# W11 pieces copied on chip into the down projection's running sum, and two W21 pieces added by GpSimd

## What is computed

```python
for l in range(DEPTH):
    x = x + hybrid_mixer(x, ...)
    x = x + conv_ffn(x, ffn_norm[l], w_up[l], conv_w[l], conv_b[l], w_down[l])
return rms_norm(x, final_norm)

def conv_ffn(x, norm_g, w_up, conv_w, conv_b, w_down):
    ...
    return (jax.nn.silu(a) * b) @ w_down      # (512, 2816) @ (2816, 1024)
```

## Time and profile before

| | |
|---|---|
| median of 3 runs | 1578.74 us (1578.1 to 1582.06) |
| time of the profiled execution | 1583.04 us |
| its span, first to last instruction | 1581.2 us |
| TensorE busy | 1563.6 us (99%) |
| VectorE, ScalarE, GpSimd busy | 74%, 49%, 16% |
| mean granted TensorE clock | 0.997 |
| DMA moved | 231.41 MB, 146 GB/s over the span |

### The profile page before, as it was taken

How to read it: one execution, slowest core, us unless ns; L and a number is a source line. 1 busy time by engine, 2 the same in 40 slices (tenths; PEclk the granted TensorE clock), 3 DMA queues, 4 the chain that set the end, 5 groups by cost and what they waited for, 6 DMA issues and landing times.

```text
span 1581.2 us, 22764 instructions
## 1 busy us (share of the span) xinstructions
PE 1563.6 (99%) x9106; PEld 1379.8 (87%) x9106; DVE 1163.5 (74%) x1295; ACT 768.9 (49%) x982; POOL 250.8 (16%) x270
## 2 busy tenths in 40 slices
PE   9999999999999999999999999999999999999988
PEld 7888888888888999999988888888888899999866
DVE  7257876786679787796972678667766897777967
ACT  5344334542355555663533533355422565556636
POOL 4000000000230222331240000000002212223400
PEclk9999999999999999999999999999999999999999
DMA  5342222222227888999133422222223388888991
GB/s 195 97 122 78 78 81 93 80 68 93 93 94 239 240 240 241 280 224 275 67 104 97 120 78 76 75 92 80 68 93 101 103 248 235 238 241 275 231 267 53
DMA packets 66628, 231.41 MB, mean 146 GB/s; under 512 B 7392, under 2 KB 7904, under 8 KB 66528
## 3 DMA queue, kind: packets, MB, share of 16 engines
q1 hardware_dynamic: 52272, 182.93, 33.7%
q0 software_dynamic: 12096, 41.95, 14.6%
q10 hardware_dynamic: 2160, 5.12, 1.2%
HBM read 225.78 MB, written 2.10 MB: 144 GB/s over the span
## 4 chain that ended last, share of the span: by engine, by line
PE 91%; DMA 4%; issue 2%; DVE 1%; POOL 1%; ACT 0%; DVEq 0%; POOLq 0%
PE ps L1762 18%; PE ps L1764 18%; PE ps L1763 18%; PE ps L1768 10%; PE ps L1770 10%; PE ps L1769 10%; DMA far_raw<-wdn 2%; PE ps L1891 1%; DMA w_raw<-wdn 1%; PE ps L1880 1%; PE ps L1858 1%; PE ps L1862 1%; DMA w_raw<-wts 1%; DMA far_raw<-wts 1%; POOL g_raw L727 1%
## 5 line engine op out<-in xcount | busy, mean ns | idle before, releaser
L1762 PE MATMUL ps<-u_hi,w_hi 128*128 128x512 f32 x768 | 301.3, 392 | 0.0
L1763 PE MATMUL ps<-u_lo,w_hi 128*128 128x512 f32 x768 | 299.3, 390 | 0.0
L1764 PE MATMUL ps<-u_hi,w_lo 128*128 128x512 f32 x768 | 299.1, 389 | 0.0
L1200 DVE TENSOR_TENSOR w_lo<-w_raw,w_hi 128x1024 fp32r<-128x1024 f32 x158 | 208.5, 1332 | 68.3 <-ACT w_hi L766 68.1
L766 ACT ACTIVATE w_hi<-w_raw 128x1024 fp32r<-128x1024 f32 x158 | 164.1, 1052 | 77.3 <-DMA w_raw<-wts 70.9
L1764 PEld LDWEIGHTS ps<-u_hi,w_lo 128*128 128x128 f32 x768 | 144.2, 188 | 30.4
L1762 PEld LDWEIGHTS ps<-u_hi,w_hi 128*128 128x128 f32 x768 | 144.4, 188 | 28.4
L1763 PEld LDWEIGHTS ps<-u_lo,w_hi 128*128 128x128 f32 x768 | 144.4, 188 | 28.3
L1768 PE MATMUL ps<-comb_hi,far_hi 128*128 128x256 f32 x576 | 161.1, 280 | 0.6 <-DVE far_lo L1363 0.2
L1769 PE MATMUL ps<-comb_lo,far_hi 128*128 128x256 f32 x576 | 160.8, 279 | 0.0
L1770 PE MATMUL ps<-comb_hi,far_lo 128*128 128x256 f32 x512 | 142.9, 279 | 0.0
(11 more groups left out here) (307 smaller groups left out, 3715.8 us busy)
## 6 DMA issues: line engine op xcount, KB each, us to landing
w_raw<-wts SPq DMA_DIRECT2D x212, 512.0 KB, 3.5
far_raw<-wts SPq DMA_DIRECT2D x56, 512.0 KB, 4.2
t_raw<-wdn POOLq DMA_DIRECT2D x30, 512.0 KB, 9.8
w_raw<-wdn SPq DMA_DIRECT2D x24, 512.0 KB, 7.6
w_raw<-wts POOLq DMA_DIRECT2D x18, 512.0 KB, 10.5
far_raw<-wts POOLq DMA_DIRECT2D x16, 512.0 KB, 7.2
far_raw<-wdn SPq DMA_DIRECT2D x16, 512.0 KB, 8.7
t_raw<-wdn SPq DMA_DIRECT2D x10, 512.0 KB, 5.7
```

The costliest lines, as they stand in the source:

```text
L1200: nc.vector.tensor_tensor(w_lo[:, s, :], w_raw[:, s, :], w_hi[:, s, :].bitcast(F32), ALU.subtract).then_inc(s_lo, 1)
L1762: nc.tensor.matmul(dst, a_hi, b_hi, start=start, stop=False)
L1763: nc.tensor.matmul(dst, a_hi, b_lo, start=False, stop=False)
L1764: return nc.tensor.matmul(dst, a_lo, b_hi, start=False, stop=stop)
```

## The change

ScalarE copies each W11 piece from the slot of its unit 0 to 5 into `t_raw` (inside `unit_high`, ahead of the high copy), and SyncE's second load of W11 is gone. GpSimd's W12 addition of piece j now waits for that copy. The W21 addition of pieces 0 and 1 is no longer a DMA: GpSimd adds the raw pieces of units 18 and 19 (W21, in slots 0 and 2) to `t_raw` by its own `tensor_tensor`. As the low part overwrites the raw piece, VectorE's low parts of units 18 and 19 wait for that sum.

```diff
+KEPT = 2
...
+        def sums_before(l, j):
+            return l * 16 * (3 + (j >= KEPT))
...
-            def load_sum(l, j):
-                sp.dma_start(t_raw[:, j, 0:piece(j)], wdn[l * 4 + W11, :, j * 1024:j * 1024 + piece(j)]).then_inc(s_tland[int(j > 1)], 16)
...
             def load_down(l):
                 done = 7 * (l * SPLIT + SPLIT - 1)
                 load_unit(l, 0)
                 for k in range(3):
                     sp.wait_ge(s_prod, done + k + 1)
-                    load_sum(l, 2 * k)
-                    load_sum(l, 2 * k + 1)
                     load_unit(l, k + 1)
                 sp.wait_ge(s_prod, done + 4)
...
             def first_sums(l):
                 for j in range(PIECES):
-                    pool.wait_ge(s_tland[int(j > 1)], l * (32 + 32 * (j > 1)) + 32 + 32 * (j > 1))
+                    pool.wait_ge(s_tcopy, l * PIECES + j + 1)
                     add_piece(l, j, W12)
             def further_sums(l):
-                for k, quarter in ((1, W22), (2, W21)):
-                    for j in range(PIECES):
-                        pool.wait_ge(s_qlo, l * UNITS_DOWN + k * PIECES + j + 1)
-                        add_piece(l, j, quarter)
+                for j in range(PIECES):
+                    pool.wait_ge(s_qlo, l * UNITS_DOWN + PIECES + j + 1)
+                    add_piece(l, j, W22)
+                for j in range(KEPT):
+                    u = 3 * PIECES + j
+                    pool.wait_ge(s_qlo, l * UNITS_DOWN + 2 * PIECES + j + 1)
+                    pool.wait_ge(s_fetch[RAW_SLOT[l][u]], 16 * (1 + l * arrivals_of_layer(u) + arrivals(u)))
+                    nc.gpsimd.tensor_tensor(t_raw[:, j, :], t_raw[:, j, :], unit_raw(l, u), ALU.add).then_inc(s_third, 1)
+                for j in range(KEPT, PIECES):
+                    pool.wait_ge(s_qlo, l * UNITS_DOWN + 2 * PIECES + j + 1)
+                    add_piece(l, j, W21)
                 for j in range(PIECES):
                     u = 4 * PIECES + j
                     s = RAW_SLOT[l][u]
-                    pool.wait_ge(s_tsum[j], l * 64 + 48)
+                    pool.wait_ge(s_tsum[j], sums_before(l, j) + 16 * (2 + (j >= KEPT)))
...
             def unit_high(l, u):
                 k, j = divmod(u, PIECES)
-                if k in (1, 2, 6):
-                    act.wait_ge(s_tsum[j], l * 64 + {1: 16, 2: 32, 6: 48}[k])
+                if k == 6 and j < KEPT:
+                    act.wait_ge(s_third, l * KEPT + j + 1)
+                elif k in (1, 2, 6):
+                    act.wait_ge(s_tsum[j], sums_before(l, j) + {1: 16, 2: 32, 6: 48}[k])
                 elif k == 4:
-                    act.wait_ge(s_tsum[j], l * 64 + 64)
+                    act.wait_ge(s_tsum[j], sums_before(l + 1, j))
                 else:
                     act.wait_ge(s_fetch[RAW_SLOT[l][u]], 16 * (1 + l * arrivals_of_layer(u) + arrivals(u)))
                 if before(HI_SLOT[l], u) is None:
                     act.wait_ge(s_prod, 7 * (l * SPLIT + SPLIT - 1) + HI_AFTER[u])
                 else:
                     act.wait_ge(s_unit, l * UNITS_DOWN + before(HI_SLOT[l], u) + 1)
+                if k == 0:
+                    act.wait_ge(s_prod, 7 * (l * SPLIT + SPLIT - 1) + j // 2 + 1)
+                    nc.scalar.activation(t_raw[:, j, 0:piece(j)], unit_raw(l, u), ACT.Copy).then_inc(s_tcopy, 1)
                 nc.scalar.activation(slot_hi(HI_SLOT[l][u])[:, 0:piece(j)], unit_raw(l, u), ACT.Copy).then_inc(s_qhi, 1)
...
                 dve.wait_ge(s_qhi, l * UNITS_DOWN + u + 1)
+                if k == 3 and j < KEPT:
+                    dve.wait_ge(s_third, l * KEPT + j + 1)
```

More of the change, by code:

```diff
@@ L403, in trunk @@
         s_c22 = sem("s_c22")
-        s_tland = [sem(f"s_tland{j}") for j in range(2)]
+        s_tcopy = sem("s_tcopy")
+        s_third = sem("s_third")
         s_tsum = [sem(f"s_tsum{j}") for j in range(PIECES)]
```

## The result

The changed kernel takes 1587.0 us, the median of 11 runs (1581.56 to 1591.15), against 1579.99 us of the kernel before on the same chips (11 runs, 1577.73 to 1585.45). The ratio is 1.0044 with a 95% interval of 1.0032 to 1.0057: 7 us slower. The forecast was 1575.0 us and no change; 1587.0 lies outside its range. The profiled execution of the changed kernel took 1589.15 us with a span of 1587.3 us, 6.1 us more than before.

What follows compares the result with a forecast made beforehand. TensorE was taken as the bound, with 11.9 us of waits and clock loss to win. Terms -1.0, -1.7 and -1.1 made -3.8 us, from the runs' median 1578.74 to 1575.0 us, range 1567.5 to 1582.0.

Steps and rivals of the forecast that it cites:

- What bounds the kernel: TensorE's waits in the down projections, 8.5 us, plus 3.4 us of clock loss: 11.9 us at most to be had.
- The copies at the seam: ScalarE's copies delay last_quarter 3.7 us and conv 2.1 us; new stall at unit 4, 1.1 us layer 0, 0.4 layer 1.
- The sums on GpSimd: Two sums of 4.1 us each cost VectorE 4.3 us; new stall at unit 14, 1.2 us layer 0, 0.9 layer 1.
- The failed step: Layer 0, product 4: half the engines per queue, so unit 28 starts at about 751.0 instead of 752.07, gaining 1.0 us.
- the new stalls of 2.3 us: Layer 0 waits of TensorE ahead of units 4 and 14, claimed as 1.1 and 1.2 us.
- So the new stalls lie inside the old one and cost nothing beyond it: Layer 0: TensorE by itself reaches unit 28 at 750.5, before its data at about 751.0, so the stalls add nothing.
- the clock's 1.7 us: Layer 0, behind unit 28: clock loss counted as won with fewer and shorter gaps ahead of it, 1.7 us.
- -1.0: Layer 0, product 4: unit 28 starts at about 751.0 instead of 752.07, a gain of 1.0 us.
- The third, layer 1: Layer 1, product 4: the last addition comes 1.2 us sooner, hence -1.1 us, with the clock left as it is.
- The second: Product 4: sums take VectorE's and the queue's time, unit 28 2.5 us later in each layer, 1584 us; chance 0.14.
- its point of decision: On GpSimd: the chain gets later if piece 4 and its followers leave past 722 us.
- The first, full relief: Product 4: all waits and clock loss go, -11.9 less up to 3.6 of new stalls, 1567 to 1570 us; chance 0.36.

Runs made afterwards that it cites:

- memset: Changed kernel with a memset, which reads nothing, in place of each of GpSimd's two sums, that part of the computation left out; ratio 0.9973.
- the seven profiles of the table above: Layer 0 of the kernel before, the changed kernel twice, and variants with three memsets per sum, copies alone, sums alone, one sum; unit 26 waits none to 4.74 us.
- copies-only kernel: Changed kernel with ScalarE's copies alone, all six W21 additions being DMAs again; ratio 1.0010.
- the later one: Second profile of the unaltered changed kernel, run again beside the experiments against the kernel before; ratio 1.0053.
- the kernels without reading sums on GpSimd: Changed kernel with memsets for GpSimd's sums, or two or six W21 sums on VectorE, with or without copies; ratios 0.9982 to 0.9962.
- the four profiles with the short lead: Changed kernel twice, sums without copies, and one sum: additions for units 24, 25 leave 6.1 to 6.4 us ahead of unit 26's load; ratios 1.0027 to 1.0053.
- the upper three: Kernel before, changed kernel with three memsets per sum (0.9982), and with copies alone (1.0010); additions for units 24, 25 lead unit 26's load by 9.0 to 10.5 us.
- the fifth product's additions first: Changed kernel with the adding DMAs for units 24 and 25 moved ahead of GpSimd's two sums in its queue; ratio 0.9986.
- six sums on VectorE: Kernel before, without copies, with all six W21 additions done by VectorE ahead of the low parts of units 18 to 23; 1573.33 us, ratio 0.9962.

## Why the prediction was wrong

**What bounds the kernel** held: the loss and the gains lie in TensorE's waits in the down projections and in the clock behind them. Two readings were off. The 8.5 us were called those of the whole program; the list has 2.5 us more, outside the down projections. And the profile that I worked from had a mean clock of 0.997, while the kernel of before mostly runs at 0.999 (median of 97 runs): I took 1.7 us of clock off the median of the runs, most of which had little of that loss to give back.

**The copies at the seam** were priced rightly, if not to the unit. last_quarter was said to slip to 677.8 us; it started at 679.23, and 1.7 us of that is the earlier difference. ScalarE, then VectorE's first conv:

```profile
677.33 1.04 ACT L888 ACTIVATE t_raw<-far_raw 128x1024 f32<-128x1024 f32 x1
...
679.23 0.57 ACT L861 ACTIVATE ca<-ps 128x512 f32<-128x512 f32 x1
...
679.88 1.52 ACT L869 ACTIVATE cc<-ca,pars 128x512 f32<-128x512 f32 x2
```

```profile
680.73 0.75 DVE L1412 SCALAR_TENSOR_TENSOR cc<-ca,pars,cc 128x512 f32<-128x512 f32 x1 [1.84 <-ACT cc L869]
```

Conv was 3.6 us later, 1.9 us without that difference, where I said 2.1. The wait was 0.87 us (I said 1.1) and stood at unit 6, as the hold by GpSimd's last product fell on the low part of unit 5 instead of unit 4; in layer 1 there was none (I said 0.4).

**The sums on GpSimd** took 3.4 us each (I took 4.1) and held VectorE for 2.2 us each, 4.4 in all (I said 4.3). The wait at unit 14 was 1.60 and 0.52 us (I said 1.2 and 0.9). The Trainium skill (SBUF — State Buffer, "Who interferes with whom") says that a VectorE operation with two SBUF inputs contends with a GpSimd one that reads, not with one that only writes. The trace agrees on both sides: 3.44 us beside a sum, 1.22 us beside a memset.

**The failed step** is this: "With half the engines each, the load for unit 26 lands at about 731.5 instead of 733.1, its addition starts when that for unit 25 is through, at about 734.5, and the one for unit 28 lands at about 747.5 instead of 748.7." The times at which the DMAs leave were right (units 24 and 25 near 720, plus 1.7: measured 721.49). What happened to them then was not. The load for unit 26 landed after 10.55 us, at 738.5, and its addition at 747.7, so that unit 26 and not unit 28 was the late one. Even by my own numbers the step was too short: that load leaves when unit 18 is done, so the new stalls of 2.3 us delay it too, from 724.03 to 726.3 (measured 727.92, less the 1.7), and landing at 731.5 would take 5.2 us where it took 9.05 before. And I had it land 3 us ahead of the addition for unit 25; in each of the seven profiles of the table above it lands 0.5 to 1.8 us behind it. The error is in the sharing. Where both queues have work, these are the windows 720 to 725 and 721 to 736 of the changed kernel (packets, MB, share of the engines' time):

```profile
q0 software_dynamic: 171, 0.63, 67.4%
q1 hardware_dynamic: 147, 0.54, 32.3%
...
q0 software_dynamic: 597, 1.92, 66.0%
q1 hardware_dynamic: 619, 2.01, 37.8%
```

Nearly equal bytes, and so two thirds of the time for the adding queue, which needs 2.5 us for 512 KB where the plain one needs 1.3. The plain queue beside it moves 2.01 MB in 15 us, 3.9 us for 512 KB (4.9 us by the first window), and not the 2.6 us of my working. Short windows are less even: in the copies-only kernel 725 to 730 shows 0.60 and 0.82 MB, but 232 and 228 packets. The Trainium skill (DMA: Bandwidth & Descriptors, "Queues, rings and completion order") says that each engine takes turns between its queues packet by packet. The trace agrees in the counts of packets, 597 and 619. From the rows alone I should have estimated 2.5 + 1.3 = 3.8 us a load, one of each kind being served in turn. With the plain loads that slow, every adding DMA that is still in the queue when the load for unit 26 is issued counts, and the two that had been 10.5 us ahead of it were 6.4 us ahead.

**"So the new stalls lie inside the old one and cost nothing beyond it"** failed with it, and so did the clock's 1.7 us, counted as won in layer 0: the loss grew to 3.4 us. So of the three terms, -1.0, -1.7 and -1.1 us, the first two came out with the wrong sign. The third, layer 1, came out even in this profile, and 0.7 us slower in the later one (698.7 us from the same ScalarE operation to the end, where it was 698.0).

**The rivals.** The second, the chain getting later, is what came true; I gave it 0.14 and 1584 us. Its sign was right, and so nearly was its condition that the addition for unit 25 is through only at 738 (737.7); but it had unit 28 late, and its point of decision was not right: the last of these DMAs, for unit 25, left GpSimd at 722.03, 720.4 without the earlier difference, and what goes with the loss is the lead over the end of unit 18. The first, full relief, comes true in part in the kernels without reading sums on GpSimd: 3 to 6 us (0.9982 to 0.9962), where it had 9 to 12.

**What stays open.** Why the addition for unit 26 itself takes 8.0 to 8.8 us with the short lead and 5.9 to 6.9 in the upper rows of the table is not shown. In layer 0 of the four profiles with the short lead the load for unit 30 leaves within 0.4 us of it (739.41 and 739.00 in the changed kernel), in the upper three 1.7 to 3.9 us behind it; but with the fifth product's additions first it takes 8.2 us too, that load leaving 4.6 us behind. No run separates this, nor why the clock falls behind some waits and not behind others of the same length (1.78 us before, 1.61 us in copies only). The layer 1 part of the loss differs between two profiles of the same kernel (3.34 and 4.75 us at unit 26), and which is typical is not known. Whether moving the two adding DMAs is worth something without any sum on GpSimd is open too.

## What to carry to other kernels

Where two DMA queues share the engines, reckon first with equal bytes, as these two had over 15 us, so that a plain load beside an adding one pays for both; and look how far ahead of the next critical load the adding transfers leave. Work that is put into an in-order queue can delay what stands behind it in two ways, by its own time and, here the larger part, through another engine that it holds, so transfers that could have left earlier are to be placed ahead of it. A sum of two SBUF tiles on GpSimd is not free for a VectorE that is short of slack: here it cost VectorE more (2.2 us) than doing the sum itself (1.22 us) in a place where it was idle.

## What the runs showed of the hardware that was not expected

TensorE's pace for 256-column matmuls differs between executions at a granted clock of 1.00: over the stretch 716 to 732 us the mean distance of two starts was 0.1187 us in the profile of before, 0.1167 in that of the changed kernel, 0.1134 with the fifth product's additions first and 0.1201 with six sums on VectorE. It is not a property of the kernel: a second profile of the changed kernel has 0.1133 us there. Differences of 1 to 5% in such stretches could make up the spread of the runs (1577.73 to 1585.45 for the kernel before, 0.5%), but the cause of the pace, and whether it is that, is not shown.
